# Weight halves ahead of the other work in the first layer's projections, and a reordered final norm

## What is computed

```python
def rms_norm(x, g):
    y = xf * lax.rsqrt(jnp.mean(xf * xf, axis=-1, keepdims=True) + EPS)
    return y * g

def mixer(h, ...):
    z = h @ p['w_in'][l]                       # 1024 -> 2560 columns
    gb, gc, xa, xb, gate = split(z)            # 512 columns each
    ya, new_conv_buf = causal_dwconv(gc * xa, conv_buf, w_short_conv)
    ya = gb * ya
    xc, new_lru_buf = causal_dwconv(xb, lru_buf, w_lru_conv)
    xc = xc + b_lru_conv
    yb, new_h = rg_lru(xc, lru_h, ...)         # two 64x64 block products, sigmoids, a scan over time
    yb = yb * jax.nn.gelu(gate)
    return concat([rms_norm(ya), rms_norm(yb)]) @ p['w_mix_out'][l], ...

def memory_kv(mem, g_mem, w_k, w_v):
    m = rms_norm(mem, g_mem)
    return m @ w_k, m @ w_v

# per layer: x += mixer(norm(x)); x += cross_attn(norm(x), k, v); x += swiglu or top-2-of-8 experts
y = rms_norm(x, norm_final)
```

## Time and profile before

| | |
|---|---|
| median of 3 runs | 1032.88 us (1032.79 to 1035.61) |
| profiled execution, its own time | 1033.01 us |
| its span, first to last instruction | 1031.2 us |
| TensorE busy | 1014.5 us, 98% of the span |
| VectorE busy | 555.7 us, 54% |
| ScalarE busy | 385.5 us, 37% |
| GpSimd busy | 102.2 us, 10% |
| granted TensorE clock, mean | 0.997 of full speed |

### The profile page before, as it was taken

One profiled execution on the slowest core, in us unless ns is written; L12 is line 12 of the kernel. 1 busy time (PEld: TensorE's weight loads), 2 busy tenths in 40 slices (PEclk: granted clock), 3 DMA queues, 4 the chain that ended last, 5 costly groups with the idle time before them and its releaser, 6 DMA issues.

```text
span 1031.2 us, 25089 instructions
## 1 busy us (share of the span) xinstructions
PE 1014.5 (98%) x10837; PEld 810.9 (79%) x10837; DVE 555.7 (54%) x980; ACT 385.5 (37%) x580; POOL 102.2 (10%) x123
## 2 busy tenths in 40 slices
PE   8899999999999999999999999999999999999996
PEld 8899999799999999999999888445544654554454
DVE  6899765588666655677977455213310331231144
ACT  6786452365555444357645145100100010010003
POOL 4113120020000001101312112000000000000000
PEclk9999999999999999999999999999999999999999
DMA  9545769756555653454668968799999999999997
GB/s 342 177 158 193 260 269 383 317 176 204 169 197 167 243 200 124 139 199 137 228 218 354 387 266 336 285 426 373 398 372 395 352 400 395 384 374 369 396 376 310
DMA packets 37808, 295.20 MB, mean 286 GB/s; under 512 B 4464, under 2 KB 4720, under 8 KB 9040
## 3 DMA queue, kind: packets, MB, share of 16 engines
q1 hardware_dynamic: 35504, 284.54, 73.0%
q0 software_dynamic: 2208, 9.23, 2.8%
HBM read 287.14 MB, written 6.58 MB: 285 GB/s over the span
## 4 chain that ended last, share of the span: by engine, by line
PE 91%; DVE 3%; ACT 2%; issue 1%; POOL 0%; POOLq 0%; DVEq 0%; ACTq 0%
PE ps L2137 33%; PE ps L1686 16%; PE ps L1687 16%; PE ps L1688 16%; PE ps L1939 1%; PE ps L1973 1%; PE ps L1959 1%; PE ps L1913 1%; PE ps L2173 1%; PE ps L2149 1%; PE ps L1831 1%; DVE wlo L1063 1%; ACT whi L663 1%; PE ps L2083 0%; PE ps L1949 0%
## 5 line engine op out<-in xcount | busy, mean ns | idle before, releaser
L1063 DVE TENSOR_TENSOR wlo<-raw,whi 128x1024 fp32r<-128x1024 f32 (+1 forms) x178 | 235.8, 1342 | 80.0 <-ACT whi L663 79.8
L1686 PE MATMUL ps<-a_hi,whi 128*128 128x264 f32 x928 | 266.6, 287 | 4.2 <-DVE wlo L1063 2.8
L1687 PE MATMUL ps<-a_lo,whi 128*128 128x264 f32 x928 | 263.8, 284 | 0.0
L1688 PE MATMUL ps<-a_hi,wlo 128*128 128x264 f32 x928 | 263.7, 284 | 0.0
L663 ACT ACTIVATE whi<-raw 128x1024 fp32r<-128x1024 f32 (+1 forms) x178 | 190.5, 1083 | 134.1 <-PE ps L1688 125.8
L1686 PEld LDWEIGHTS ps<-a_hi,whi 128*128 128x128 f32 x928 | 175.6, 189 | 6.5 <-DVE wlo L1063 3.1
L1687 PEld LDWEIGHTS ps<-a_lo,whi 128*128 128x128 f32 x928 | 175.5, 189 | 0.3
L1688 PEld LDWEIGHTS ps<-a_hi,wlo 128*128 128x128 f32 x928 | 174.8, 188 | 0.0
L2137 PE MATMUL ps<-raw,xg 128*32 128x352 f32 x1536 | 116.6, 460 | 0.0
L2137 PE MATMUL ps<-wide,xg 128*32 128x352 f32 x1536 | 115.1, 459 | 0.0
L2137 PEld LDWEIGHTS ps<-wide,xg 128*32 128x32 f32 x1536 | 50.2, 110 | 63.4 <-issue 63.4
(11 more groups left out here) (320 smaller groups left out, 1558.1 us busy)
## 6 DMA issues: line engine op xcount, KB each, us to landing
raw<-dense_in_dram SPq DMA_DIRECT2D x58, 1024.0 KB, 5.0
raw<-moe_in_dram SPq DMA_DIRECT2D x36, 1408.0 KB, 9.6
wide<-moe_in_dram SPq DMA_DIRECT2D x36, 1408.0 KB, 10.4
raw<-gu_in_dram SPq DMA_DIRECT2D x22, 1024.0 KB, 4.8
raw<-moe_in_dram SPq DMA_DIRECT2D x12, 1536.0 KB, 8.8
wide<-moe_in_dram SPq DMA_DIRECT2D x12, 1536.0 KB, 9.4
raw<-cache_in_dram SPq DMA_DIRECT2D x12, 1024.0 KB, 8.4
wcache<-cache_in_dram SPq DMA_DIRECT2D x12, 1024.0 KB, 7.1
```

The source lines that it names most:

```text
L1063: dve.tensor_tensor(wlo[m % 4][:, 0:w], raw[:, k % RAWS, c:c + w], whi[m % 4][:, 0:w].bitcast(f32), ALU.subtract).then_inc(lo_done, 1)
L1686: pe.matmul(out, w_hi, m_hi_, start=first, stop=False)
L1687: pe.matmul(out, w_hi, m_lo_, start=False, stop=False)
L1688: return pe.matmul(out, w_lo, m_hi_, start=False, stop=last)
```

## The change

In the steps of layer 0, ScalarE makes both high parts of a chunk ahead of the step's body, and VectorE makes the second low part directly behind the evacuation and ahead of the step's extra. In layer 1 and elsewhere the order stays. At the end, TensorE sums the folded squares behind those of tiles 4, 5 and 6 and ahead of 7; ScalarE applies the gain to tiles 0 to 3 ahead of the root and to 4 to 7 behind it; VectorE scales four pairs instead of four single tiles and two pairs.

```diff
-            def step(off, k, body=None, split=True):
+            def step(off, k, body=None, split=True, weights_first=False):
                 if split:
                     hi(off, k + 2, 0)
+                if split and weights_first:
+                    hi(off, k + 2, 1)
                 if body:
                     body()
-                if split:
+                if split and not weights_first:
                     hi(off, k + 2, 1)
...
                 for j in range(10):
-                    step(0, IN + j, do.get(j), split=l or j)
+                    step(0, IN + j, do.get(j), split=l or j, weights_first=l == 0)
...
+            def gained(ks):
+                for k in ks:
+                    c = PK["g_fin"] + k
+                    act.activation(hf[:, k], x[:, k], ACT.Copy, scale=pk[:, 0, c:c + 1]).then_inc(fin_g, 1)
+
+            gained(range(4))
             root("fin", 1.0 / D)
-            for k in range(4, KT):
-                c = PK["g_fin"] + k
-                act.activation(hf[:, k], x[:, k], ACT.Copy, scale=pk[:, 0, c:c + 1]).then_inc(fin_g, 1)
+            gained(range(4, KT))
...
                 dve.wait_ge(pe_done, off * 2 + (2 * k + 2))
                 read().then_inc(evac, 1)
+                if split and weights_first:
+                    lo(off, k + 2, 1)
                 if extra:
                     dve.wait_ge(evac, off + (k + 1))
                     extra()
                 if late:
                     lo(off, k + 2, 0)
-                if split:
+                if split and not weights_first:
                     lo(off, k + 2, 1)
...
                     step(0, IN + j, scaled_in(j), (lambda: [fn() for fn in extras[j]]) if j in extras else None,
-                         split=l or j)
+                         split=l or j, weights_first=l == 0)
...
             root_reciprocal("fin")
-            for k in range(4):
-                dve.scalar_tensor_tensor(out=hf[:, k], in0=x[:, k], scalar=col(0, "g_fin", k), in1=rstd[:],
-                                         op0=ALU.mult, op1=ALU.mult).then_inc(n_h, 1)
-            for k in (4, 6):
-                dve.wait_ge(fin_g, k - 2)
+            for k in (0, 2, 4, 6):
+                dve.wait_ge(fin_g, k + 2)
                 dve.tensor_tensor(hf[:, k:k + 2], hf[:, k:k + 2], over_pair(rstd), ALU.mult).then_inc(n_h, 2)
...
             pe.wait_ge(n_rt, order["fin"])
-            for k in (4, 0, 5, 6, 7):
+            for k in (4, 5, 6, 0, 7):
```

More of the change, by code:

```diff
@@ L1068, in banks, with step @@
                 return ps[:, b:b + 2, 0:w]
-            def step(off, k, read, extra=None, first=None, split=True, late=False):
+            def step(off, k, read, extra=None, first=None, split=True, late=False, weights_first=False):
                 if first:
```

## The result

The changed kernel takes **1040.25 us** (median of 6 runs, 1038.28 to 1041.12) against 1032.97 (6 runs, 1031.60 to 1035.61) before it: ratio **1.0064 [1.0048, 1.0079]**, the medians 7.3 us apart. The profiled execution took 1041.12 us, 8.1 more than the one before.

A forecast was written before the change was run, and what follows sets the result against it. TensorE, 91% of the span, was taken to bound the kernel. From the profiled 1033.01, -4.5 + 8.35 + 1.5 - 1.15 = +4.2 gave 1037.21, put at 1037.1 us for the median; 8-in-10 range 1034.2 to 1039.0.

The forecast's parts named there:

- What is removed: At chunk 3 (256 weight columns), TensorE's 3.0 us stall for VectorE's low part and the 1.5 slow stretch behind it go.
- Term 1: Chunk 4: TensorE waits for VectorE's evacuation of chunk 2, behind the taps and one low part; +0.65 us.
- The cover: VectorE's idle time before the convolution taps hides chunk 3's early low part; without it taps start 1.64 us later.
- Term 2: First gate matmul pair, mid chunk 5: TensorE waits for ScalarE's memory-norm root, now behind a waiting high part; +1.65 us.
- Term 3: Second gate pair, behind chunk 5: TensorE waits for two sigmoids, now behind ScalarE's high part; +3.45 us.
- Term 4: Values chunks: VectorE's low part for chunk 13 comes 2.95 later, slack 0.35; +2.6 us, bounds 0 and 3.6.
- The clock: TensorE runs slow behind the new 3.45 us gap, as behind the old 3.0 one; +1.5 us, bounds 0 and 3.0.
- The tail: Final norm: root starts 0.85 us sooner, four scaled pairs and transfers save 0.3; -1.15 us, bounds 0.4 and 1.4.
- The table loads: ScalarE: a switch of function table costs about its load's 1.28 us.
- The chain to chunk 13 has slack: Rival, chance 0.13: the values-chunks wait is nothing and the clock holds; 1033.0 us, losses eat the gain.
- the waits hide: Rival, chance 0.03: the waits at both gate pairs and chunk 13 vanish; 1027.9 us, faster.
- More stretches: Rival, chance 0.04: more slow-clock stretches, or the chain to chunk 13 later still; 1039 us and above.

The follow-up runs named there:

- tail only: Changed kernel with layer 0's old weights order put back, only the new final norm kept: 1032.41 us, 0.9987 of the kernel before.
- 5 alone: Kernel before the change, with the new order in step 5 of layer 0 only and the old final norm: 1038.79 us, 1.0055.
- front only: Changed kernel with the old final norm put back, layer 0's new weights order kept: 1040.60 us, 1.0072 of the kernel before.
- Not 4, 5: Changed kernel with steps 4 and 5 of layer 0 back in the old order, new final norm kept: 1032.99 us, 0.9994.
- not 7-9: Changed kernel with steps 7 to 9 of layer 0 back in the old order, new final norm kept: 1037.74 us, 1.0040.

## Why the prediction missed

**What is removed (-4.5): right.** Chunk 3's gap and its slow stretch (18 matmuls started at PEclk 0.50, where the next window has 30) are gone. From the start to the end of chunk 3 the shift goes from -0.3 to -4.95, a gain of 4.65.

**Term 1 (+0.65): measured 1.3.** TensorE's idle time is 1.06; from start to start it loses 1.3: the matmuls on either side of the gap start 1.34 apart (33.08 and 34.42) and the next one 0.23 later, where without a gap they start 0.12 apart. The cover, which the prediction took the old idle time to give, was not free. VectorE's early low part runs where GpSimd folds the memory's squares. GpSimd in the changed kernel, and VectorE's taps:

```profile
27.01 1.79 POOL L522 TENSOR_TENSOR sq_m<-sq_m 128x256 f32<-128x256 f32 x1
...
29.57 0.92 POOL L522 TENSOR_TENSOR sq_m<-sq_m 128x256 f32<-128x256 f32 x1
```

```profile
27.00 1.21 DVE L1069 TENSOR_TENSOR wlo<-raw,whi 128x1024 fp32r<-128x1024 f32 x1
29.32 0.58 DVE L1194 SCALAR_TENSOR_TENSOR xc<-z,pk,xc 128x255 f32<-128x255 f32 x1 [1.11 <-issue]
29.82 0.70 DVE L1197 SCALAR_TENSOR_TENSOR xc<-pk,xc 128x8 f32<-128x8 f32 x1
...
32.53 1.21 DVE L1069 TENSOR_TENSOR wlo<-raw,whi 128x1024 fp32r<-128x1024 f32 x1
```

The fold that starts with the low part takes 1.79 (0.73 with the old order, as the traces of "tail only" and "5 alone" have it too), so the last two folds run beside the taps, where only the last did before, and two of the small taps take 0.70 instead of 0.21. From the first tap to the next low part it is 3.21 us, where the earlier trace rows had 2.70. The fold started with the low part and ended 0.59 behind it (28.80 and 28.21); what held it, no run shows.

**Term 2 (+1.65): measured 1.9.** The idle time is 1.65 as forecast; from start to start it is 1.9.

**Term 3 (+3.45): measured 3.6**, free of clock effects in "front only" and "5 alone". **Term 4 (+2.6, the least certain): measured 2.7** (idle 2.44). "Not 4, 5" shows that term 3 comes from its own steps, and "5 alone" from which; of the 4.2 at chunk 13, "not 7-9" leaves 1.0. Term 4's working is in VectorE's rows, the evacuation of chunk 9 and the first product for the recurrence, in the changed kernel:

```profile
83.58 0.70 DVE L1275 TENSOR_TENSOR z<-ps,rstd 128x528 f32<-128x528 f32 x1
...
85.33 1.25 DVE L1220 TENSOR_TENSOR z<-z 128x1056 f32<-128x1056 f32 x1
```

The same product before:

```profile
79.37 1.26 DVE L1212 TENSOR_TENSOR z<-z 128x1056 f32<-128x1056 f32 x1
```

TensorE is 3.2 late there. So against TensorE the evacuation (78.63 before) came 1.7 later, where the forecast had 1.8, and the product 2.7, where it had 2.95.

**The clock (+1.5, one new slow stretch): this is the step that failed.** The prediction gave the gap of 3.45 a stretch, because it was nearest to the 3.0 that had one, and kept a second one behind the 2.6 as a bound. The price was right (1.4 to 1.6 each). The number was not: chunk 13's gap brought its own, +1.5, in every one of the four profiles in which that gap was 2.4 or more. So a gap's length did not tell which of them gets one: the longest, which had the only stretch of the sum, got it in 3 of 5 profiles, and that it came in the changed kernel's profile was in part luck. With chunk 13's stretch the sum would have been 1038.6; with the 1.15 that terms 1 to 4 were short of, less 0.15 gained beyond the 4.5, 1039.6, inside the measured runs. Of the 3.2 that the median lies above the forecast, 1.5 is thus this stretch and 1.0 the waits; the rest, 0.7, is not shown by itself. The third stretch, in the routing, adds 1.4 in the profiled execution. It came in 4 of the 10 profiles, with the front changed and without, so it is no effect shown to be the change's; the executions of the changed kernel spread from 1038.28 at a mean clock of 0.996 to 1041.12 at 0.994 (one of 1039.51 had 0.997, so the mean clock does not order them alone).

**The tail (-1.15): measured -0.9 at the final sums, and 0.3 more to the end.** Right.

**The table loads.** The prediction took a switch at its 1.28, and the changed kernel shows the same: the load at 51.50 takes 1.28, and the sigmoid behind it starts at 52.80, 0.02 after its end.

**The rivals.** "The chain to chunk 13 has slack" and "the waits hide" are refuted by the idle times. "More stretches", with 0.04, is what happened.

**What stays open.** Why the gate pair's gap of 3.31 had a slow stretch in 3 profiles and not in 2 others: in the three it began at 50.4 to 50.6 us, in the two at 51.8 and 52.2, and no run tests whether that matters. And what sets off the stretch in the routing, and the idle times of 0.6 to 1.4 us near 820, which come in some executions of several of these kernels.

## What to carry to other kernels

An operation moved to the head of an in-order queue brings its wait along, and everything behind it inherits that wait (here ScalarE's 4.16 us ahead of the high part at 50.43, with the sigmoids behind it that TensorE then waited 3.31 for): before moving it, ask what it waits for, and whether the engine it waits for needs what now stands behind it. Do so step by step: here three of the nine steps hold the front's gain, and the other six, taken together, brought the losses (VectorE's part of step 5, taken alone, gained 0.8). Price a new gap together with the clock behind it, for each gap by itself.

## What the runs showed of the hardware

- The gap of 2.4 us at chunk 13 came with 3.41 us at half clock (0.50) in 4 of 4 profiles, the one of 2.84 at chunk 3 in 3 of 3, that of 3.31 at the gates in 3 of 5, and those of 0.78, 1.06 and 1.65 in none. So the longest of them was not the surest in these few profiles. In 5 of the 10 the clock fell 0.2 to 0.6 us before the gap had ended, in the other 5 it fell 0.4 to 1.5 us behind it.
- In the routing, TensorE fell to half clock for 3.41 us in 4 of 10 profiles, at 1.2 to 1.4 us each; ahead of it in the changed kernel was only an idle time of 0.69, which stands in all ten.
- Beside a GpSimd product, two low parts of VectorE took 4.66 us instead of 2.35, and one fold of GpSimd beside a low part took 1.79 instead of 0.73.
